# Second block's mixer as one stage: projection in pieces between attention and recurrence, weights through one ring

## Chip, cores and metric

One core of a Trainium2 chip runs the whole program: two transformer blocks of a first model, then one block of a second one, then a norm. The metric is the time of the program on the device in microseconds (us), the median of several executions.

## What is computed

The input is 256 tokens by 1024 features in float32, and all arithmetic is float32. The change touches the mixer of the last block. Cut to what matters:

```python
h = rmsnorm(x, attn_norm)
proj = h @ w_in                               # 1024 x 5400
q, kv, gate, hg_q, hg_f, hg_i, hg_g, merge = split(proj)
# 8 heads of 64, 2 key groups; three branches over all 256 keys or 15 compressed ones
k_cmp, v_cmp = rope(compress(k, w_cmp_k)), compress(v, w_cmp_v)
o_nsa = g0*softmax(q k_cmp)v_cmp + g1*softmax(q k_slc)v_slc + g2*softmax(q k_win)v_win
# gated recurrence, 4 heads, keys and values 128 wide, chunks of 64 tokens
f = lb + (1 - lb) * sigmoid(hg_f);  k = 1 - f;  state = f*state + k v
o_hg = rmsnorm(q . state, hg_norm) * silu(hg_g)
mixed = sigmoid(merge[0]) * (o_nsa @ w_br_nsa) + sigmoid(merge[1]) * (o_hg @ w_br_hg)
x = x + mixed @ w_out
```

A mixture of 32 experts follows, as in the two blocks before it.

## The kernel before

Tokens lie as two tiles of 128 partitions (`TILES`). The program is a row of stages. Each ends in `Stage.close`, which waits for all engines, so nothing of one stage overlaps the next but the loads that a stage issues ahead. A float32 matmul of the program is two matmul instructions in the trace; a transpose is one. PE is TensorE, DVE VectorE, ACT ScalarE, SP the engine that issues the loads.

The mixer is this row of stages in `program`:

- `norm_stage` "s_norm1": `h` and its transpose `hT`. SP loads the first two of twelve 450-column blocks of `w_in` and the two masks `levels` and `causal`, and waits for the masks.
- `project_stage` (matmuls L1115): 12 blocks of columns by 2 tiles by 8 chunks of features, copies out of PSUM by DVE (L1139) and ACT (L1130). Two weight slots.
- `rope_stage` (DVE), `turn_stage` (transposes L1021), `compress_stage` (matmuls L1845) with `Forget` beside it; PE's first transpose there waits for `w_cmp_k` and `w_cmp_v`, loaded in the stage itself.
- `attend_stage`: 12 units (3 branches by 2 tiles by 2 groups of 4 heads). A unit is: scores on PE (L1365), scale and bias on DVE (L1408), row maximum (L1412), exponentials on ACT (L1383), transposes of the probabilities (L1343), their copy by ACT (L1394), the product with v (L1355), then the division and gates on DVE (L1425 to L1434), which sums the branches in SBUF.
- `turn_stage`, then `hgrn_stage`: cumulative sums (L1660, L1663), chunk updates (L1669), seven levels of products within a chunk (L1680) whose factors DVE prepares (L1729, L1730, L1737, L1738) and whose results it masks and adds up (L1747, L1752), then the outputs (L1687, L1692).
- `head_norm_stage`, `turn_stage`, `project_stage` for `w_br_nsa`, again for `w_br_hg`, `turn_stage`, and `project_stage` for `w_out`, which adds to `x` and issues the first loads of the experts.

Of the kernel before, what the change touches and what calls it, by code (L numbers as in the profile page):

```python
# [40 lines left out]
class Stage:  # L41
# [4 lines left out]
    def __init__(self, nc, name):  # L46
        self.nc, self.name, self.sems = nc, name, []
# [677 lines left out]
class NormWeight:  # L725
# [9 lines left out]
    def wait(self, eng):  # L735
        eng.wait_ge(self.landed, 16 * self.n)
# [1142 lines left out]
    arena.at = mark  # L1879


def program(nc, ins, const_dram, out, dump=None):

    psum = nc.alloc_psum_tensor("psum", [P, 4096], F32)
# [14 lines left out]
    def experts_of(tag, names, layer):  # L1899

        stage, mem = Stage(nc, tag), alloc_moe(arena, norm_tile)
        return stage, mem, Experts(stage, mem, extra_slot(arena), *(ins[n][layer] for n in names))
# [6 lines left out]
    def normed(tag, scale=None, shift=None, loads=None, ready_too=None, chunked=False):  # L1909
        norm_stage(nc, tag, x, h, norm_w, scale, shift, hT, ident, banks, loads=loads, ready_too=ready_too, chunked=chunked)  # L1910
# [5 lines left out]
    def ahead_of(plan, w_row):  # L1916
        def loads(sp):
            norm_w.fetch(sp, w_row)
            plan[2].prefetch(sp)
        return loads  # L1920
# [95 lines left out]
        arena.at = 0  # L2016


    mark = arena.at
    arena.take([WEIGHTS])  # L2020
    N = ins["w_in_2"].shape[2]
    in_columns = Columns(nc, "s_in", ins["w_in_2"][0], DC, N // 12, arena, at=mark)
    consts["levels"], consts["causal"] = arena.take([896]), arena.take([TOK])
    later_landed = whole.sem("later_consts")

    def first_loads(sp):
        in_columns.fetch(sp)
        for n in LATER:
            sp.dma_start(consts[n], const_dram[n]).then_inc(later_landed, 16)
        sp.wait_ge(later_landed, 16 * len(LATER))  # L2030

    normed("s_norm1", loads=first_loads)
    out_columns = Columns(nc, "s_out", ins["w_out_2"][0], DC, 512, arena, at=mark)
    nsa_columns = Columns(nc, "s_brn", ins["w_br_nsa_2"][0], DC // 2, 512, arena)
    o = arena.take([TILES, D])
    pr = arena.take([TILES, N])
    project_stage(nc, in_columns, hT, pr, arena, banks)
    kv = pr[:, :, 512:1280].rearrange("p t (s g d) -> p t s g d", s=6, g=2)
    hk, g = arena.take([TILES, 512]), arena.take([TILES, 512])
    mark2 = arena.at  # L2040
    half = ROPE_DIM // 2
    rope = consts["rope"][:, :].rearrange("p (t n) -> p t n", t=TILES)
    heads = lambda ap: ap.rearrange("p (n d) -> p n d", d=64)
    jobs = []
    for t in range(TILES):
        cs = (rope[:, t, 0:half], rope[:, t, half:])
        jobs += [(heads(pr[:, t, 0:512]), *cs), (kv[:, t, 2], *cs), (kv[:, t, 4], *cs)]
    rope_stage(nc, "s_rope", jobs, arena)
    qT, cT = arena.take([HEADS, TOK], parts=64), arena.take([4, TOK], parts=64)
    ksT, kwT = arena.take([2, TOK], parts=64), arena.take([2, TOK], parts=64)  # L2050
    turn_stage(nc, "s_turn", [(pr[:, :, 0:512], 64, 8, qT), (pr[:, :, 512:768], 64, 4, cT), (pr[:, :, 768:896], 64, 2, ksT),
                              (pr[:, :, 1024:1152], 64, 2, kwT)], ident, banks)
    kcT, vc = arena.take([2, N_CMP], parts=64), arena.take([2, 64], parts=N_CMP)
    hq, hf, hi, hg = (pr[:, :, 1304 + i * 512:1304 + (i + 1) * 512] for i in range(4))
    compress_stage(nc, "s_cmp", cT, ins["cmp_pos_2"][0], ins["w_cmp_k_2"][0], ins["w_cmp_v_2"][0], kcT, vc, consts, arena, banks,
                   beside=lambda st: Forget(nc, st, ins["hg_lb_logits_2"], hf, hf, hk, g, (pr[:, :, 1280:1304], pr[:, :, 3352:]),
                                            arena))
    gates = pr[:, :, 1280:1304].rearrange("p t (h i) -> p i t h", i=3)
    cb = consts["cmp_bias"][:, :].rearrange("p (t n) -> p t n", t=TILES)
    cm = consts["cmp_mask"][:, :].rearrange("p (t n) -> p t n", t=TILES)  # L2060
    o_nsa = o[:, :, 0:512]
    nsa = dict(qT=qT, hd=64, kv_of=lambda hh: hh // 4, scale=64 ** -0.5, out=o_nsa)
    some = cm[:, :, 0:1]
    attentions = [dict(nsa, kT=kcT, v=lambda kt, g_: vc[:, g_, :], keys=N_CMP,
                       bias=lambda t, hs, nk: cb[:, t, :].unsqueeze(1).to_broadcast([P, HEADS // 2, N_CMP]),
                       factors=[lambda t, hs: gates[:, 0, t, hs], lambda t, hs: some[:, t, :].to_broadcast([P, HEADS // 2])])]
    for i, (kk, s) in enumerate(((ksT, 3), (kwT, 5))):
        attentions.append(dict(nsa, kT=kk, v=lambda kt, g_, s=s: kv[:, kt, s, g_, :], add=True,
                               bias=lambda t, hs, nk: consts["causal"][:, TOK - nk:].unsqueeze(1).to_broadcast([P, HEADS // 2, nk]),
                               factors=[lambda t, hs, i=i: gates[:, i + 1, t, hs]]))  # L2070
    attend_stage(nc, "s_attn", attentions, ident, arena, psum)
    if dump: dump("s_nsa", o)
    arena.at = mark2
    hqT, hkT = arena.take([HG_HEADS, TOK]), arena.take([HG_HEADS, TOK])
    turn_stage(nc, "s_hturn", [(hq, P, 4, hqT), (hk, P, 4, hkT)], ident, banks)
    o_hg = o[:, :, 512:1024]
    hgrn_stage(nc, "s_hgrn", g, hqT, hkT, hk, hi, o_hg, consts, arena, banks)
    head_norm_stage(nc, "s_hnorm", [(o_hg, 4, 128, ins["hg_norm_2"][0])], arena,
                    loads=lambda sp: (nsa_columns.fetch(sp), out_columns.fetch(sp)), gated=(hg, o_hg))
    arena.at = mark2 - 2 * TILES * 512  # L2080
    turn_stage(nc, "s_oturn", [(o, P, DC, hT)], ident, banks)
    mixed = arena.take([TILES, D])
    hg_columns = Columns(nc, "s_brh", ins["w_br_hg_2"][0], DC // 2, 512, arena)
    tmp = arena.take([TILES, 512])
    project_stage(nc, nsa_columns, hT[:, 0:4, :], mixed, arena, banks, gate=pr[:, :, 3352:3352 + D], ahead=hg_columns.fetch)
    project_stage(nc, hg_columns, hT[:, 4:8, :], mixed, arena, banks, tmp=tmp, gate=pr[:, :, 3352 + D:], add=True)
    turn_stage(nc, "s_mturn", [(mixed, P, DC, hT)], ident, banks)
    arena.at = mark
    plan = experts_of("s_moe", ("w_grp_2", "b_grp_2", "w_rtr_2", "b_rtr_2", "w_gate_2", "w_up_2", "w_down_2"), 0)
    project_stage(nc, out_columns, hT, x, arena, banks, add=True,  # L2090
                  ahead=ahead_of(plan, ins["ffn_norm_2"][0]))
    if dump: dump("s_mix", x)
    arena.at = mark
    normed("s_norm2", loads=extra_of(plan), chunked=True)
    moe(plan, None, ins["final_norm_2"])
    norm_stage(nc, "final", x, h, norm_w, None, None, store=rows(out[0]))
# [55 lines left out]
```

## Time and profile before

| | us |
|---|---|
| median of 3 runs | 2465.34 |
| lowest, highest | 2463.25, 2467.79 |
| the profiled execution's own time | 2461.11 |
| its span | 2459.1 |
| PE busy | 2065.8 |
| DVE busy | 667.0 |
| ACT busy | 358.7 |

The span is counted in the trace from its first to its last record; the execution's own time has 2 us around it. Busy time of PE is summed over the span and does not tell at which of the engine's two clock rates it ran. The three expert stages are the long even stretches of 427 to 430 GB/s in the page; the mixer of the last block lies between the second and third of them, at 1502 to 1946 us.

### The profile page before, as it was taken

To read this page: it belongs to the slowest core of one execution; us is meant where nothing else is said; L and a number is where in the kernel's file an instruction comes from. 1 tells how busy PE (TensorE), PEld (TensorE's weight loads), DVE (VectorE), ACT (ScalarE), POOL (GpSimd) and SP (SyncE) were. 2 spreads that over 40 slices of the span, in tenths; PEclk is the share of its full clock that TensorE was granted. 3 is DMA by queue.
4 is the path that set the end of the run, shared out by engine and by line. 5 is a ranking of instruction groups with operands and counts; after the bars stand their busy time and mean duration, and the time that the engine had idled before them with its cause. 6 is when DMAs were issued, how large, how long until landed. Compare 5 with 4: busy or idle time off the path is not lost. (4 is left out here: it accounts for less than half of the span.)

```text
span 2459.1 us, 29045 instructions
## 1 busy us (share of the span) xinstructions
PE 2065.8 (84%) x11243; PEld 1136.5 (46%) x11243; DVE 667.0 (27%) x1427; ACT 358.7 (15%) x736; POOL 0.3 (0%) x5
## 2 busy tenths in 40 slices
PE   6955689999896967699998886994966789999996
PEld 2634355554443425355554443543853355554442
DVE  2774321111112463411111112004462221111112
ACT  2022121111111012211111101003311121111111
POOL 0000000000000000000000000000000000000000
PEclk9965889999999988699999998996567789999999
DMA  8940949999997953489999993431003749999995
GB/s 290 366 156 11 375 181 422 427 429 427 428 430 291 325 202 146 176 359 428 428 429 428 428 428 142 156 123 27 0 1 138 319 188 423 428 428 428 429 430 243
DMA packets 135016, 732.32 MB, mean 298 GB/s; under 512 B 18736, under 2 KB 44803, under 8 KB 85659
## 3 DMA queue, kind: packets, MB, share of 16 engines
q1 hardware_dynamic: 132860, 728.14, 72.8%
q10 hardware_dynamic: 2080, 3.15, 0.4%
q8 instruction: 50, 0.82, 0.1%
q14 instruction: 26, 0.21, 0.0%
HBM read 727.06 MB, written 4.20 MB: 297 GB/s over the span
## 5 line engine op out<-in xcount | busy, mean ns | idle before, releaser
L261 PE MATMUL psum<-arena,norm_w 128*64 128x256 f32 x6144 | 708.6, 383 | 59.6 <-DMA arena<-in_moe_w_dram 21.1
L261 PEld LDWEIGHTS psum<-arena,norm_w 128*64 128x64 f32 x6144 | 436.1, 137 | 328.1 <-issue 72.1
L292 PE MATMUL psum<-arena,hT 128*64 128x512 f32 x1536 | 349.4, 596 | 22.1 <-DMA arena<-in_moe_w_dram 13.6
L361 DVE COPY hT<-psum 64x512 f32<-64x512 f32 x96 | 66.6, 694 | 780.7 <-PE psum L292 780.7
L1115 PE MATMUL psum<-arena,hT 128*128 128x450 f32 (+1 forms) x640 | 264.3, 575 | 15.9 <-DVEq L1135 15.9
L292 PEld LDWEIGHTS psum<-arena,hT 128*64 128x64 f32 x1536 | 106.1, 136 | 232.8 <-issue 215.8
L1115 PEld LDWEIGHTS psum<-arena,hT 128*128 128x128 f32 x640 | 124.1, 195 | 153.9 <-issue 147.2
L312 PE MATMUL psum<-hT 128*128 128x512 f32 x384 | 177.5, 605 | 2.5 <-ACT hT L361 2.5
L1205 PE MATMUL psum<-arena,hT 128*128 128x290 f32 (+1 forms) x448 | 149.3, 493 | 8.1 <-DMA arena<-in_even_w_in_dram 4.2
L392 ACT ACTIVATE hT<-psum 128x256 f32<-128x256 f32 x96 | 36.8, 383 | 724.6 <-PE psum L261 724.6
L548 DVE COPY hT<-psum 128x256 f32<-128x256 f32 x96 | 40.8, 425 | 322.7 <-PE psum L280 322.7
L1205 PEld LDWEIGHTS psum<-arena,hT 128*128 128x128 f32 x448 | 85.1, 191 | 71.7 <-issue 49.8
L361 ACT COPY hT<-psum 64x512 f32<-64x512 f32 x96 | 55.5, 578 | 413.7 <-PE psum L292 413.7
L312 PEld LDWEIGHTS psum<-hT 128*128 128x128 f32 x384 | 69.0, 189 | 91.3 <-issue 86.2
L691 DVE SCALAR_TENSOR_TENSOR arena<-arena,ccol 128x512 f32<-128x512 f32 x140 | 105.3, 752 | 5.0
L990 PE MATMUL psum<-const_ident,h 128*128 128x128 f32 x80 | 21.7, 433 | 61.3 <-DVEq L977 60.8
L1021 PE MATMUL psum<-const_ident,arena 128*128 128x128 f32 (+1 forms) x174 | 28.2, 335 | 43.5 <-PEq L55 43.5
L384 ACT COPY norm_w<-arena 128x512 f32 x96 | 59.5, 622 | 31.5 <-issue 29.7
L546 DVE TENSOR_TENSOR hT<-hT,psum 128x256 f32<-128x256 f32 x96 | 40.5, 422 | 54.1 <-ACT hT L392 51.2
L1343 PE MATMUL psum<-const_ident,arena 128*128 128x128 f32 (+1 forms) x112 | 25.6, 391 | 30.3 <-ACT arena L1394 24.6
L1365 PE MATMUL psum<-arena 64*128 64x128 f32 (+4 forms) x160 | 46.1, 451 | 4.4 <-PEq L55 4.4
L484 DVE TENSOR_SCALAR arena<-const_iota,arena 128x64 f32<-128x64 f32 x204 | 49.7, 308 | 0.1
(289 smaller groups left out, 1275.0 us busy)
## 6 DMA issues: line engine op xcount, KB each, us to landing
arena<-in_moe_w_dram SPq DMA_DIRECT2D x192, 2048.0 KB, 28.6
arena<-in_w_gate_dram SPq DMA_DIRECT2D x32, 2048.0 KB, 27.8
arena<-in_w_up_dram SPq DMA_DIRECT2D x32, 2048.0 KB
arena<-in_w_down_dram SPq DMA_DIRECT2D x32, 2048.0 KB, 31.7
arena<-in_ada_w_dram SPq DMA_DIRECT2D x24, 2048.0 KB
arena<-in_w_in_dram SPq DMA_DIRECT2D x12, 1800.0 KB, 7.2
arena<-in_odd_w_in_dram SPq DMA_DIRECT2D x6, 2048.0 KB, 13.4
arena<-in_even_w_in_dram SPq DMA_DIRECT2D x8, 1160.0 KB, 14.1
```

The source lines that it names most:

```text
L261: m = nc.tensor.matmul(out[64 * half:64 * half + 64, :], xw[:, u, c, :], w[:, c, half * HALF:(half + 1) * HALF], start=(c == 0), stop=(c = ...
L292: m = nc.tensor.matmul(bank_Y[64 * half:64 * half + 64, :], hTs[:, k % 2, (k // 2) * 64:(k // 2) * 64 + 64], experts.slots[slot][2][:, k, ...
L312: m = nc.tensor.matmul(bank_acc[2 * t + half][:, :], selT[:, t, :], y[:, half, :], start=False, stop=False, skip_group_check=True)
L361: return eng_copy(y[BLOCK * u:BLOCK * (u + 1), half, :], bank_Y[64 * half:64 * half + 64, :])
L384: nc.scalar.copy(xw[:, u], sorted_x[:, :, bass.ds(start, BLOCK)]).then_inc(xw_ready, 1)
L484: m = nc.vector.tensor_scalar(selw[:, t, BLOCK * u:BLOCK * (u + 1)], iota[:, 0:BLOCK], slots[:, t, bass.ds(g, 1)], comb[:, t, bass.ds(g, 1 ...
L546: nc.vector.tensor_tensor(hm, sil, H3[u], ALU.mult).then_inc(hm_ready, 1)
L548: nc.vector.tensor_copy(hTs, HT).then_inc(hT_copied, 1)
L691: m = nc.vector.scalar_tensor_tensor(out, wt[:, k, :], self.ccol[:, k:k + 1], out, ALU.mult, ALU.add)
L1115: m = nc.tensor.matmul(banks[2 * u + t][:, 0:width], inT[:, k, t * P:(t + 1) * P], wt[:, u, k, :], start=(k == 0), stop=(k == kc - 1))
L1205: m = nc.tensor.matmul(banks[2 * u + t][:, 0:width], inT[:, k, t * P:(t + 1) * P], wt[:, b % SLOTS, k, :], start=(k == 0), stop=(k == kc - 1))
L1365: m = nc.tensor.matmul(S(n, nk)[:, i, :], job["qT"][:, h, t * P:(t + 1) * P], job["kT"][:, job["kv_of"](h), 0:nk], start=True, stop=True)
```

## The change

`project_stage`, `rope_stage`, `turn_stage`, `compress_stage`, `attend_stage`, `hgrn_stage`, `head_norm_stage` and their closes are replaced for this mixer by one stage, `second_mixer_stage`. Its weights go through `Ring`: three slots, 11 blocks of `w_in` columns (ten of 512, one of 280), the two branch matrices, two halves of `w_out`. A `project(n, t)` is one block for one tile; in the loops it is cut in two parts of 4 chunks (`QUARTERS`). Queries and keys are transposed two heads at a time (keys are written twice), so that the score matmuls alternate between partitions 0 to 63 and 64 to 127. Gates and division go onto the probabilities before their transpose, the products with v come out transposed, and the three branches add up in one PSUM bank. The two masks and `w_cmp` are loaded in the stage, behind the ring's first three blocks. All copies of projections are ACT's. The diff, cut:

```diff
+IN_2 = ((512, 1024), (0, 512), (1024, 1304), (1816, 2328), (1304, 1816), (2328, 2840), (2840, 3352), (3352, 3864), (3864, 4376),
+        (4376, 4888), (4888, 5400))
+class Ring:
+    SLOTS = 3
...
+    def wait(self, pe, n):
+        pe.wait_ge(self.landed[n % self.SLOTS], 16 * (n // self.SLOTS + 1))
+def second_mixer_stage(nc, ring, x, h, hT, w, consts, arena, psum, banks, ahead):
...
+        def _(sp):
+            sp.dma_start(prow, w["pos"]).then_inc(cw_landed, 16)
+            sp.dma_start(cw[:, 0], w["cmp_k"].rearrange("(l d) o -> d l o", d=64)).then_inc(cw_landed, 16)
+            sp.dma_start(cw[:, 1], w["cmp_v"].rearrange("(l d) o -> d l o", d=64)).then_inc(cw_landed, 16)
...
+            for n in range(ring.SLOTS, OUT + 1):
+                sp.wait_ge(made[1], n - ring.SLOTS + 1)
+                ring.load(sp, n)
+            sp.wait_ge(brn_made, 4)
+            ring.load(sp, OUT + 1)
+            sp.wait_ge(mix_ready, 4)
+            ahead(sp)
...
+            pe.wait_ge(cw_landed, 48)
+            nc.tensor.transpose(banks[2][0:64, 0:CMP_LEN], prow, ident[0:CMP_LEN, 0:CMP_LEN]).then_inc(pos_turned, 1)
+            project(0, 0)
+            project(0, 1)
+            project(1, 0)
...
+            def score(u):
...
+                for j in range(4):
+                    rows = slice(64 * (j % 2), 64 * (j % 2) + 64)
+                    m = nc.tensor.matmul(S[:, (j % 2) * 2 + j // 2, 0:nk], qT[rows, 2 * s + j // 2, t * P:(t + 1) * P],
+                                         kT[rows, s, 0:nk], start=True, stop=True)
...
+            def turn_unit(u):
...
+                pe.wait_ge(normed, u + 1)
...
+            pe.wait_ge(exped, 1)
+            for n in range(len(UNITS) + 3):
+                if n >= 3:
+                    output_unit(n - 3)
+                if 2 <= n < len(UNITS) + 2:
+                    turn_unit(n - 2)
+                if n < len(UNITS):
+                    score(n)
+                project(*QUARTERS[n])
+            project(*QUARTERS[len(UNITS) + 3])
+            pe.wait_ge(decayed, 1)
+            pe.wait_ge(o_kept, 4)
...
+            for n in range(len(LEVELS) + 1):
+                compare(n)
+                project(*QUARTERS[16 + n])
+            project(*QUARTERS[23])
+            pe.wait_ge(ready, 1)
...
+        def _(act):
...
+            for n in range(len(UNITS) + 2):
+                if n >= 2:
...
+                    act.wait_ge(turned, n - 1)
...
+                    nc.scalar.copy(PT[0:wd, n % 2, 0:k, :], T[0:wd, 0:k, :]).then_inc(pt_copied, 1)
+                if n < len(UNITS):
...
+                    act.wait_ge(maxed, n + 1)
...
+                if n >= 2 and n % 2 == 0:
+                    keep(*QUARTERS[n - 1][0:2])
+            keep(*QUARTERS[13][0:2])
+            keep(*QUARTERS[15][0:2])
+            for n in range(len(LEVELS)):
+                act.wait_ge(asked, n + 1)
...
+        def _(dve):
...
+            for n in range(len(UNITS) + 3):
+                if n < len(UNITS):
+                    scale(n)
+                if 1 <= n < len(UNITS) + 1:
+                    normalise(n - 1)
+                if n >= 3 and (n - 3) % 3 == 2:
+                    keep_output((n - 3) // 3)
...
+            for n in range(last + 2):
+                if n + 1 < last:
+                    exponents(n + 1)
+                if n < last:
+                    factors(n)
+                if n == 0:
+                    carry()
+                if n:
+                    collect(n - 1)
...
-    project_stage(nc, in_columns, hT, pr, arena, banks)
...
-    attend_stage(nc, "s_attn", attentions, ident, arena, psum)
...
-    hgrn_stage(nc, "s_hgrn", g, hqT, hkT, hk, hi, o_hg, consts, arena, banks)
...
+    ring = Ring(nc, "s_mix", loads, arena, 0)
+    normed("s_norm1", loads=ring.fetch)
...
+    second_mixer_stage(nc, ring, x, h, hT, dict(
...
+        hg_norm=ins["hg_norm_2"][0], levels=const_dram["levels"], causal=const_dram["causal"]), consts, arena, psum, banks, ahead)
```

How PE's instructions stand around two attention units of 256 keys. In the kernel before, L1365 are scores, L1343 transposes, L1355 products with v:

```order
L1365 MATMUL psum<-arena 128x256 x4
L1355 MATMUL psum<-arena 128x64 x4
L1343 MATMUL psum<-const_ident,arena 128x128 x4
L1365 MATMUL psum<-arena 128x256 x4
L1355 MATMUL psum<-arena 128x64 x4
L1343 MATMUL psum<-const_ident,arena 128x128 x8
```

In the changed kernel, L2101 are scores, L2114 transposes, L2130 products with v and L2025 the projection:

```order
L2025 MATMUL psum<-arena,hT 128x512 x4
L2130 MATMUL psum<-arena 64x128 x8
L2114 MATMUL psum<-const_ident,h 15x128 x4
L2101 MATMUL psum<-arena 128x256 x4
L2025 MATMUL psum<-arena,hT 128x512 x4
L2130 MATMUL psum<-arena 64x128 x4
L2114 MATMUL psum<-const_ident,h 128x128 x8
```

Every round now holds four matmuls of 128x512, and the transposes come one round later behind the scores.

On PE in the recurrence, before: sums' updates (L1669), all levels in a row (L1680), first output:

```order
L1669 MATMUL psum<-arena 128x128 x12
L1680 MATMUL psum<-arena 128x128 x56
L1687 MATMUL psum<-arena 128x128
L1692 MATMUL psum<-arena 64x128
```

Now, with L2151 the updates and L2164 the levels:

```order
L2151 MATMUL psum<-arena 128x128 x12
L2164 MATMUL psum<-arena 128x128 x8
L2025 MATMUL psum<-arena,hT 128x512 x4
L2164 MATMUL psum<-arena 128x128 x8
L2025 MATMUL psum<-arena,hT 128x512 x4
L2164 MATMUL psum<-arena 128x128 x8
```

Between two levels there are again four matmuls of the projection.

On SP at the start of the mixer, now: three blocks in the norm stage, then what the stage itself loads before its first block is released:

```order
L1903 DMA arena<-in_w_in_dram 128x8x512 x2
L1903 DMA arena<-in_w_in_dram 128x8x280
L943 UNCONDITIONAL_BRANCH
L1996 UNCONDITIONAL_BRANCH
L1998 DMA arena<-in_cmp_pos_dram 32x64
L1999 DMA arena<-in_w_cmp_k_dram 64x32x64
L2000 DMA arena<-in_w_cmp_v_dram 64x32x64
```

The compression weights stood in a stage of their own after the whole projection; they now stand behind three blocks of the projection in the queue.

## Rows read from the trace of the kernel before

**Rows 1.** The page: busy tenths of PE and its clock in 40 slices.

```profile
PE   6955689999896967699998886994966789999996
PEclk9965889999999988699999998996567789999999
```

**Rows 2.** Stretches: us, busy of PE, PEld, DVE, ACT, POOL, clock, DMA share, GB/s.

```profile
1516.80:1665.00 148.20, 148.12 (x384) 73.77 (x384) 6.90 (x11) 5.87 (x11) 0.00 (x0) 0.98 0.36 125
1665.00:1690.00 25.00, 5.29 (x33) 4.45 (x33) 8.10 (x41) 10.11 (x10) 0.00 (x0) 0.72 0.45 61
1690.00:1710.00 20.00, 7.40 (x259) 6.93 (x258) 16.26 (x25) 3.40 (x3) 0.00 (x0) 0.50 0.01 5
1710.00:1788.00 78.00, 74.20 (x288) 62.65 (x288) 28.80 (x69) 29.14 (x109) 0.00 (x0) 0.50 0.00 1
...
1795.00:1868.00 73.00, 40.58 (x196) 33.17 (x196) 48.81 (x66) 14.37 (x18) 0.00 (x0) 0.66 0.09 32
...
1874.00:1910.00 36.00, 29.36 (x64) 12.59 (x64) 7.93 (x12) 0.00 (x0) 0.00 (x0) 0.95 0.27 104
...
1914.00:1945.40 31.40, 29.59 (x64) 12.85 (x64) 2.58 (x4) 0.00 (x0) 0.00 (x0) 0.93 0.92 356
sum 428.60, PE 344.33 PEld 215.09 DVE 124.66 ACT 66.39 POOL 0.00; mean PE 34.43 PEld 21.51 DVE 12.47 ACT 6.64 POOL 0.00
```

**Rows 3.** The same view at two loads: first blocks with masks, then w_cmp.

```profile
1503.00:1515.00 12.00, 3.81 (x16) 2.85 (x16) 4.04 (x7) 4.57 (x9) 0.00 (x0) 0.50 0.98 356
1681.00:1690.00 9.00, 0.16 (x1) 0.12 (x1) 0.00 (x0) 5.74 (x4) 0.00 (x0) 0.60 1.26 168
```

**Rows 4.** Timeline of PE, the compression: start, us, group, idle before.

```profile
1689.84 0.26 PE L1840 MATMUL psum<-const_ident,arena 32*64 32x32 f32 x1 [11.81 <-DMA arena<-in_w_cmp_v_dram]
1694.37 7.02 PE L1845 MATMUL psum<-arena 64*15 64x64 f32 x256 [4.28 <-DVEq L1862]
```

**Rows 5.** Groups by shape, attention of the last block: busy us, mean ns, idle before.

```profile
L1383 ACT ACTIVATE arena<-arena 128x256 f32<-128x256 f32 x16 | 7.9, 497 | 19.1 <-DVE arena L1412 19.1
L1408 DVE SCALAR_TENSOR_TENSOR arena<-psum,arena 128x1024 f32<-128x1024 f32 x4 | 4.9, 1225 | 12.5 <-PE psum L1365 12.5
L1394 ACT COPY arena<-psum 128x1024 f32<-128x1024 f32 x4 | 4.0, 1000 | 7.7 <-PE psum L1343 7.7
```

**Rows 6.** Attention of the second block (heads of 128): its clock, then PE's timeline.

```profile
936.00:954.00 18.00, 12.04 (x88) 10.90 (x88) 8.27 (x12) 8.69 (x30) 0.00 (x0) 1.00 0.00 1
...
936.71 1.89 PE L1365 MATMUL psum<-arena 128*128 128x256 f32 x8
...
943.84 1.06 PE L1343 MATMUL psum<-const_ident,arena 128*128 128x128 f32 x8 [2.18 <-ACT arena L1394]
...
948.49 3.74 PE L1355 MATMUL psum<-arena 128*128 128x128 f32 x32
```

**Rows 7.** Timeline of PE: one row half at a time, row halves in turn, column halves in turn.

```profile
1747.90 2.07 PE L1365 MATMUL psum<-arena 64*128 64x128 f32 x8
...
221.03 2.24 PE L1528 MATMUL psum<-arena 64*128 64x128 f32 x16 [4.11 <-DVEq L1570]
...
1439.47 3.67 PE L261 MATMUL psum<-arena,norm_w 128*64 128x256 f32 x32 [1.08 <-DMA arena<-in_moe_w_dram]
```

**Rows 8.** The recurrence: DVE's first and last of the levels, PE's last two levels.

```profile
1806.93 0.69 DVE L1729 TENSOR_TENSOR arena<-arena 128x512 f32<-128x512 f32 x1
...
1837.72 3.84 PE L1680 MATMUL psum<-arena 128*128 128x128 f32 x32 [0.98 <-DVEq L1739]
...
1844.58 1.23 DVE L1752 TENSOR_TENSOR arena<-arena 128x1024 f32<-128x1024 f32 x1
```

**Rows 9.** Timeline of PE: the turn after the head norm, the second branch.

```profile
1868.62 3.65 PE L1021 MATMUL psum<-const_ident,arena 128*128 128x128 f32 x16 [12.16 <-PEq L55]
...
1892.43 13.97 PE L1115 MATMUL psum<-arena,hT 128*128 128x512 f32 x32 [2.60 <-DVEq L1135]
```

More of the change, by code:

```diff
@@ L1879, in compress_stage, with __init__, tile, load @@
     arena.at = mark
+IN_2 = ((512, 1024), (0, 512), (1024, 1304), (1816, 2328), (1304, 1816), (2328, 2840), (2840, 3352), (3352, 3864), (3864, 4376),
+        (4376, 4888), (4888, 5400))
+class Ring:
+    SLOTS = 3
+    def __init__(self, nc, tag, loads, arena, at):
+        self.stage, self.loads = Stage(nc, tag), loads
+        self.wt = arena.view([self.SLOTS, DC * 512], at, P)
+        self.landed = [self.stage.sem(f"w{u}") for u in range(self.SLOTS)]
+    def tile(self, n, kc, width):
+        return self.wt[:, n % self.SLOTS, 0:kc * width].rearrange("p (c n) -> p c n", c=kc)
+    def load(self, sp, n):
+        src = self.loads[n]
+        kc, width = src.shape[0] // P, src.shape[1]
+        sp.dma_start(self.tile(n, kc, width), src.rearrange("(c p) n -> p c n", p=P)).then_inc(self.landed[n % self.SLOTS], 16)
+    def fetch(self, sp):
+        for n in range(self.SLOTS):
+            self.load(sp, n)
+    def wait(self, pe, n):
+        pe.wait_ge(self.landed[n % self.SLOTS], 16 * (n // self.SLOTS + 1))
@@ L2016, in program @@
         arena.at = 0
[L2019 to L2036, printed above, removed]
-    project_stage(nc, in_columns, hT, pr, arena, banks)
[L2038 to L2070, printed above, removed]
-    attend_stage(nc, "s_attn", attentions, ident, arena, psum)
-    if dump: dump("s_nsa", o)
-    arena.at = mark2
-    hqT, hkT = arena.take([HG_HEADS, TOK]), arena.take([HG_HEADS, TOK])
@@ L2075, in program @@
-    turn_stage(nc, "s_hturn", [(hq, P, 4, hqT), (hk, P, 4, hkT)], ident, banks)
-    o_hg = o[:, :, 512:1024]
-    hgrn_stage(nc, "s_hgrn", g, hqT, hkT, hk, hi, o_hg, consts, arena, banks)
[L2078 to L2089, printed above, removed]
@@ L2090, in program, with ahead @@
-    project_stage(nc, out_columns, hT, x, arena, banks, add=True,
-                  ahead=ahead_of(plan, ins["ffn_norm_2"][0]))
+    w_in = ins["w_in_2"][0]
+    loads = [w_in[:, a:z] for a, z in IN_2] + [ins["w_br_nsa_2"][0], ins["w_br_hg_2"][0]]
+    loads += [ins["w_out_2"][0][:, i * 512:(i + 1) * 512] for i in range(2)]
+    ring = Ring(nc, "s_mix", loads, arena, 0)
+    normed("s_norm1", loads=ring.fetch)
+    arena.at = ring.SLOTS * DC * 512
+    plans = []
+    def ahead(sp):
+        at, arena.at = arena.at, 0
+        plans.append(experts_of("s_moe", ("w_grp_2", "b_grp_2", "w_rtr_2", "b_rtr_2", "w_gate_2", "w_up_2", "w_down_2"), 0))
+        arena.at = at
+        ahead_of(plans[0], ins["ffn_norm_2"][0])(sp)
```

506 lines of the change are left out of this document (505 added, 1 removed).

## The prediction

> **What bounds the kernel now.** I read the page's slices first [rows 1]: each is 61.5 us, and while experts run PE has 8 or 9 tenths and nearly full clock. In the 28th to 32nd slice, 1660 to 1967 us, it has 4, 9, 6, 6 and 7 tenths, and the clock 6, 5, 6, 7 and 7. Next the stretches of that mixer [rows 2]. From its first projection matmul at 1516.8 us to DVE's last add at 1945.4 it takes 428.6 us; PE is busy in 344.3 of them, DVE in 124.7, ACT in 66.4. No other engine is near PE, so two things can be won: the 84.3 us in which PE idles, and the part of its busy time that only a low clock makes. The clock column shows where that is. The projection has 0.98 (1.2 and 2.4 GHz are the two levels, 0.5 and 1.0): 148.12 us for 2 tiles of 5400 columns. Compression and attention stand at 0.50, where PE is "busy" 74.2 of 78 us; the recurrence has 0.66, with PE busy 40.6 of 73 and DVE 48.8. Branches and output again have 0.93 to 0.95. DMA has a share of 0.36 in the projection's stretch, so weights do not bound it.
>
> That attention's busy time is clock and not work is seen in the second block, where the granted clock was 1.00 although PE was busy only 12.0 of 18 us [rows 6]: there eight score matmuls of 128x256 take 1.89 us, eight transposes 1.06, 32 products of 128x128 3.74. Those are my prices at full clock: 0.24, 0.13 and 0.12 us an instruction.
>
> **The change, part by part.** I cost it as PE's list in order of time, at full clock, with the waits that stay; DVE and ACT are the cover to be tested.
>
> *Start.* Before, the norm stage waits for two blocks and the masks: 356 GB/s over 12 us, 4.27 MB [rows 3]. Now it fetches three blocks, 5.3 MB, and waits for none. But PE's first instruction waits for `w_cmp` behind them. In the kernel before, those loads held PE 11.8 us [rows 4], most of it in a stretch where 168 GB/s were moved for 9 us [rows 3]. At that pace I put about 8.5 us behind the ring's blocks, which themselves take some 15 us from 1502.5: PE begins at 1526 instead of 1516.8. Bounds: 1521 if the two kinds of load share the queues' time, 1530 if they run one after the other at the old wait's 11.8. The cost is 9 us, open from 4 to 13.
>
> *Phase 1, blocks 0 to 4.* Their projection is 2328 of the 5400 columns: 2328/5400 x 148.1 = 63.9 us [rows 2]. Moved between them: 42 transposes at 0.13 = 5.5; compression, 256 instructions in 7.0 as before [rows 4]; the cumulative sums 3.7 (16 instructions of 128 columns at 0.12, four of 512 at the 0.437 of 13.97/32 [rows 9]); 2.3 waiting for their exponentials on ACT (one pass of 1024 columns takes 1.0, as the copy L1394 does [rows 5]); 1.5 for a dip of the clock at the small compression matmuls. Sum 84. The rope, the forget gate and the copies hide under 8-matmul groups of 7 us; the separate stages from 1665 to 1710, 45 us of which PE used 12.7, and their closes disappear.
>
> *Phase 2, attention.* 14 rounds up to the last output, each with a quarter of four 128x512 matmuls, hence two instructions each: 8 x 0.437 = 3.5 [rows 9], 14 x 3.5 = 49.1. Work of attention: 64 transposes x 0.13 = 8.3; outputs, 128 instructions of 128 columns, 11.5; scores 12. The last two have bounds. Scores in one row half at a time took 2.07 us for 8 instructions of 128 columns at half clock, so 0.13 at full, and 256 columns twice that; with row halves in turn 16 took 2.24, 0.14 each at half clock [rows 7]: alternation nearly halves it. All pairs overlapping gives 7.7, none 15.4; I take the middle, as only one layout of two is alike. Outputs alternate column halves; the nearest row, 32 of 256 columns in 3.67, is 0.115 each [rows 7], which says overlap; 0.06 for 128 columns gives 8, no overlap 15.4, and I take 11.5. Sum 81, bounds 75 to 88.
> Beside it the Trainium skill, page "TensorE: Matmul & The Clock Gate", section "Part 3: Packing small matmuls — row/col tiling", says that matmuls in different row groups run at the same time, their weight loads overlapping. By that rule scores would be 7.7 and this phase 4 us shorter; the trace agrees for row halves with 0.14 against 0.26.
>
> What covers it: at 256 keys DVE needs scale 1.22, maximum 1.22, normalisation (a pass of 1024 like them) 1.23 and three small ones of some 0.2, together 4.3; ACT four exponentials of 0.50 and a copy of 1.0, and half a copy of a projection [rows 5]. The score of unit n is followed by a quarter and an output before the transposes that wait for the normalisation of unit n-1: 3.5 + 1.4 = 4.9 us of PE. So DVE is hidden by about 0.6 us, in the four units of 256 keys only; the eight smaller units have over 1.5. The fetch of a 2.1 MB block, 5.9 us at the 356 GB/s of [rows 3], hides under the 14 us that a block's matmuls last.
>
> *Phase 3, recurrence.* Two quarters 7.0, updates 24 at 0.12 = 2.8; seven levels and the diagonal. In each, 16 instructions; 32 of them took 3.84 at the better clock [rows 8], so 1.92 a level, 13.4 for seven; eight quarters 28.1; 2 waiting for DVE. Sum 53. DVE's levels from first to last took 38.9 [rows 8], partly waiting for ACT and PE; per level DVE has four passes of 0.69 and two masks and an add, about 5.4, as much as PE's 1.92 + 3.5. This cover is thin as well, hence the 2.
>
> *Phase 4.* Last products of the recurrence, 40 at 0.12 = 4.8; first branch 14.0; 4 transposes and a copy 1.4; second branch 14.0 [rows 9]; turn and copies 2.3; output 28.0; second turn 1.0; add 0.8. Sum 66.3. The head norm, where PE idled 12.2 us before L1021 [rows 9], now runs on ACT and DVE under the first branch, about 14 us against 14: the cover just reaches. The experts' first loads still start some 31 us ahead of the end, as before at 1914, so the next stage keeps its start.
>
> Sum 84 + 81 + 53 + 66.3 = 284.3, and 3 us for some thirty hand-overs among engines that I did not price singly. 1526 + 287.3 = 1813.3, against 1945.4: 132.1 us less. Of these about 84 are idle time, less the 9 of the start and 7 of waits that stay, and the other 60-odd are PE's work at full instead of half clock. The profiled execution's own time was 2461.1 and becomes 2329.0; the median of the runs is 4.2 above it, so the forecast is **2333**.
>
> **Rivals.**
> *B, the hand-overs bind.* PE waits in each round for DVE's normalisation or ACT's copy, as it waited 2.18 us for L1394 even at full clock [rows 6]. For it: covers of 0.6 us, and `link` waits between DVE's small operations. Against: only four units are of 256 keys. Price 2.18 x 12 = 26: 2359.
> *C, the clock stays at 1.2 GHz in part of the rounds.* For it: all attention of this mixer ran at 0.50 although PE was busy 95% of the time [rows 2], and rounds of this kind alternate banks and wait. Against: the second block's attention had 1.00 with gaps [rows 6], and half of each round is the projection that had 0.98. If half of phase 2 is at half clock, 40 us: 2373. The Trainium skill, same page, section "A second HAM failure mode: psum-queue depth-cycling", describes a clock that falls again and again in a kernel that cycles PSUM banks; by it the time would be this one.
> *D, the other side.* Interleaving pulls the projection down with attention instead of the reverse: phases 2 and 3 wholly at half clock. Their 134 us double; the gain of 132 is gone and the kernel takes 2467 or a little more. It decides from 132 us of PE's work at half rate. Against it speaks the same row of the projection, and that PE has fewer gaps than before.
> *E, it doesn't do what it says.* Blocks arrive late from a ring of three and PE stands at every block, so that the work is still serial: about 2465. It takes 12 us lateness per block; the fetch rate of [rows 3] says 5.9 us for each.
>
> **Chances.** Forecast 0.62, own range 2318 to 2350 (start 4 to 13, phase 2 75 to 88, some 8 us either way on thin covers). B 0.20, C 0.13, D 0.03, E 0.02. The range reaches down to 2313, as all terms at their low ends give, and up through B and C to 2385; about 0.1 lies outside, D and E among it. A measurement of this kernel can tell about 0.2%, 5 us, from no change: A, B and C are all faster, 0.95; E is the same, 0.02; D slower, 0.03.
>
> **What would show it.** PE's first instruction of the stage at 1526 right after a wait for `w_cmp`. A clock of 1.0 from the first block to some 1810, with at most a dip at compression. Rounds of 7 to 8 us around units of 256 keys, and of 5 to 6 around others, with idle PE below 0.3 us in each; B would show as idle before the transposes with DVE's normalisation as what ended it, C as quarters of 7 us and not 3.5. Levels of 5.4 to 5.8 us. The first branch without a gap behind it, and the stage's last add at about 1813. The forecast is wrong if this add comes after 1830 or the clock in the rounds lies under 0.8.

## The result and the profile after

The changed kernel takes 2325.5 us, the median of four executions, against 2464.9: the ratio is 0.943, interval 0.941 to 0.945. One of the four took 6232 us; nothing in the later runs is like it, its cause is not known, and it is left out of the ratio, though not out of the median (the other three have 2321.7). Timed once more beside another kernel it took 2317.4 (0.941, 0.939 to 0.942), so 139 to 145 us are saved, where 132 had been forecast. The profiled execution took 2329.4.

The page of the changed kernel, busy tenths of PE and its clock in 40 slices (now 58.2 us each), answers to [rows 1]:

```profile
PE   7955769999988696768999988869999799999886
PEclk9975769999999898869999999979999799999999
```

The mixer lies in the 27th to 32nd slice (from 1513 us). The clock has 7 tenths in the first of them, with the wait at the start, 9 in the four after it, and 7 in the last, most of which lies behind the mixer. The stretches by the four phases of the prediction answer to [rows 2] (same columns):

```profile
1537.42:1620.70 83.28, 78.82 (x480) 42.18 (x480) 23.55 (x52) 16.83 (x27) 0.00 (x0) 0.96 0.38 136
1620.70:1697.45 76.75, 76.75 (x400) 40.11 (x401) 32.96 (x70) 32.99 (x117) 0.00 (x0) 1.00 0.24 84
1697.45:1748.97 51.52, 49.67 (x218) 29.72 (x217) 35.70 (x50) 8.27 (x10) 0.00 (x0) 1.00 0.23 82
1748.97:1815.75 66.78, 64.47 (x193) 30.61 (x191) 16.70 (x25) 13.60 (x16) 0.00 (x0) 1.00 0.59 226
sum 278.33, PE 269.71 PEld 142.62 DVE 108.91 ACT 71.69 POOL 0.00; mean PE 67.43 PEld 35.65 DVE 27.23 ACT 17.92 POOL 0.00
```

From PE's first instruction to DVE's last add the mixer lasts 278.3 us where it had lasted 428.6. PE idles 8.6 of them and not 84.3, and is busy 269.7 and not 344.3, half the gain each way: 75.7 us of idle time and 74.6 of busy time. The clock is 1.00 through attention and recurrence, where it had been 0.50 and 0.66. DVE is busy 15.8 us less than before (108.9 us) and ACT 5.3 more (71.7); their work now lies beside PE's.

The timeline of PE in the changed kernel (start, us, group, idle before) at the stage's start, in the rounds around units of 256 keys, and in the levels:

```profile
1519.35 3.81 PE L990 MATMUL psum<-const_ident,h 128*128 128x128 f32 x16 [11.89 <-DVEq L977]
1537.42 0.25 PE L2039 MATMUL psum<-const_ident,arena 32*64 32x32 f32 x1 [14.26 <-DMA arena<-in_w_cmp_v_dram]
...
1580.67 1.41 PE L2058 MATMUL psum<-arena 64*15 64x64 f32 x87 [2.20 <-issue]
...
1620.70 0.62 PE L2101 MATMUL psum<-arena 64*128 64x15 f32 x8 [2.26 <-ACT arena L2269]
...
1661.29 0.66 PE L2130 MATMUL psum<-arena 128*64 128x128 f32 x8
1661.88 0.61 PE L2114 MATMUL psum<-const_ident,h 128*15 128x128 f32 x4
1662.42 1.13 PE L2101 MATMUL psum<-arena 64*128 64x256 f32 x8
1663.48 3.70 PE L2025 MATMUL psum<-arena,hT 128*128 128x512 f32 x8
1667.11 0.65 PE L2130 MATMUL psum<-arena 15*64 15x128 f32 x8
1667.70 1.09 PE L2114 MATMUL psum<-const_ident,h 128*128 128x128 f32 x8
...
1714.11 2.05 PE L2164 MATMUL psum<-arena 128*128 128x128 f32 x16 [1.03 <-DVEq L2468]
1716.00 3.60 PE L2025 MATMUL psum<-arena,hT 128*128 128x512 f32 x8
1719.44 1.95 PE L2164 MATMUL psum<-arena 128*128 128x128 f32 x16
...
1821.31 4.89 PE L990 MATMUL psum<-const_ident,h 128*128 128x128 f32 x16 [6.28 <-DVEq L977]
```

Read it so: after the norm's transposes PE waits 14.3 us for the load of `w_cmp`, then runs without a gap but for 2.2 us in the middle of the compression matmuls, for which the profile shows no cause, 2.3 at the first scores, 0.8 and 1.0 in the levels, and 0.3 and 1.3 behind the branches. From one round's products to the next it is 5.8 us in the rows shown, and 5.8 to 6.7 in the four rounds with scores of 256 keys, with no idle time shown. The distance from the norm's first transpose (L990) to that of the next norm is the measure used below: it holds the mixer with both its ends, 302.0 us here, 302.3 in the second profile of the same kernel, and 444.5 in the kernel before (1506.94 to 1951.41). So the stage gives 142.5 us. In the first profile it merely began 12.4 us later than before; in the second, 2.2 us later (1509.10). Those 10 us are the difference between the two executions (2329.4 and 2319.6). They arise in the earlier stages, which are the same in all kernels here, and in whose profiles the norm begins anywhere from 1502.6 to 1519.4 us; what causes that is not known.

### The profile page after: what moved, and what is told of

Read it like the earlier page. It is cut to its first block and busy times, and to the rows that moved or that the text cites. A ratio compares the mean times of both kernels' runs of the same rounds, so it can differ in the third digit from the quotient of the medians.

```text
span 2327.6 us, 28443 instructions
## 1 busy us (share of the span) xinstructions
PE 2002.0 (86%) x11195; PEld 1070.3 (46%) x11195; DVE 651.3 (28%) x1387; ACT 364.0 (16%) x748; POOL 0.3 (0%) x5
## 5 line engine op out<-in xcount | busy, mean ns | idle before, releaser
L2025 PE MATMUL psum<-arena,hT 128*128 128x512 f32 (+1 forms) x352 | 154.8, 590 | 0.0
L1205 PEld LDWEIGHTS psum<-arena,hT 128*128 128x128 f32 x448 | 86.0, 193 | 72.5 <-issue 51.3
L2025 PEld LDWEIGHTS psum<-arena,hT 128*128 128x128 f32 x352 | 65.8, 194 | 69.0 <-issue 66.8
L990 PE MATMUL psum<-const_ident,h 128*128 128x128 f32 x80 | 21.7, 434 | 60.2 <-DVEq L977 59.8
L1115 PE MATMUL psum<-arena,hT 128*128 128x512 f32 x128 | 57.3, 609 | 3.5 <-DVEq L1135 3.5
L716 PE MATMUL psum<-arena,const_ones 128*128 128x512 f32 x40 | 24.3, 773 | 26.1 <-PEq L55 26.1
L990 PEld LDWEIGHTS psum<-const_ident,h 128*128 128x128 f32 x80 | 14.3, 217 | 69.7 <-DVEq L977 69.7
## 6 DMA issues: line engine op xcount, KB each, us to landing
arena<-in_odd_w_in_dram SPq DMA_DIRECT2D x6, 2048.0 KB, 13.1
```

What stands on the lines that cost most here:

```text
L1115: m = nc.tensor.matmul(banks[2 * u + t][:, 0:width], inT[:, k, t * P:(t + 1) * P], wt[:, u, k, :], start=(k == 0), stop=(k == kc - 1))
L1205: m = nc.tensor.matmul(banks[2 * u + t][:, 0:width], inT[:, k, t * P:(t + 1) * P], wt[:, b % SLOTS, k, :], start=(k == 0), stop=(k == kc - 1))
L2025: m = nc.tensor.matmul(banks[t][:, 0:width], hT[:, k, t * P:(t + 1) * P], ring.tile(n, DC, width)[:, k, :], start=(k == 0), stop=(k == DC ...
```

## Experiments

All are edits of the changed kernel. "Stage" is the distance between the two norms' first transposes, 302 us in the changed kernel.

**The projection taken out of the rounds.** Three kernels: everything ahead of the attention; only the levels alone; only the attention alone.

```diff
+            for q in range(0, 24):
+                project(*QUARTERS[q])
             pe.wait_ge(exped, 1)
             for n in range(len(UNITS) + 3):
...
-                project(*QUARTERS[n])
-            project(*QUARTERS[len(UNITS) + 3])
...
-                project(*QUARTERS[16 + n])
-            project(*QUARTERS[23])
```

(ACT's copies moved in the same way; in the second kernel quarters 16 to 23 stand ahead of the updates, in the third quarters 0 to 15 ahead of the attention.)

> All of the projection stands before the attention, nothing of it between rounds or levels. Theory 1 (the gain is that the chains of DVE and ACT run beside the projection, and the clock stays up because PE is never idle): attention alone takes some 55 us with PE idle for a third or more of it, the recurrence some 40, so the stage grows by 55 - 28 + 40 - 16 = about 50 us, 2375. Theory 2 (the clock alone: attention by itself keeps PE busy, only at 1.2 GHz): attention stands at clock 0.5 with PE busy over 90%, about 56 us, and the recurrence loses little: 2355. Theory 3 (the merged stage and the new layout make the gain, interleaving little): within 10 us of the changed kernel, 2335 or less.

> Projection between the attention rounds as in the change, but the last eight quarters ahead of the levels. Theory 1: levels are bound by DVE's 5.4 us a level, 40 us for seven with PE idle 3 of each 5, against 16 beside the projection: the stage from its first matmul to DVE's last add grows from 278 to about 300 us. Theory 3: by under 5 us.

> Sixteen quarters ahead of the attention, the last eight between the levels. Theory 1: the stage grows from 278 to about 305 us, attention takes about 55 us, and the two losses (this one and that of the levels alone) add up to that of the kernel with everything first. Theory 2: attention at clock 0.5 and PE busy over 90%. In both the clock recovers in the levels.

Everything first: 2383.0 us, ratio 0.967 (0.966 to 0.969), stage 363.6, 61.6 more. Levels alone: 2344.3, stage 329.4, 27.4 more. Attention alone: 2360.7, stage 337.7, 35.7 more; the two add up to 63 (these two, and all kernels below but those of the start, were executed once, so I compare them by their stage). Stretches of the kernel with everything first, attention and then the levels, columns as above:

```profile
1692.44:1757.41 64.97, 42.81 (x289) 31.03 (x289) 30.89 (x69) 28.91 (x109) 0.00 (x0) 0.66 0.09 33
...
1757.41:1792.19 34.78, 23.53 (x136) 21.77 (x136) 31.62 (x46) 13.68 (x11) 0.00 (x0) 0.71 0.00 0
```

And PE's timeline there, at the end of the projection and the first rounds, then around units of 256 keys:

```profile
1609.94 82.56 PE L2025 MATMUL psum<-arena,hT 128*128 128x512 f32 x192
...
1696.45 0.61 PE L2114 MATMUL psum<-const_ident,h 128*15 128x128 f32 x4 [2.25 <-DVE h L2424]
1696.99 1.21 PE L2101 MATMUL psum<-arena 64*128 64x128 f32 x8
...
1718.34 2.08 PE L2101 MATMUL psum<-arena 64*128 64x256 f32 x8
...
1730.43 1.97 PE L2114 MATMUL psum<-const_ident,h 128*128 128x128 f32 x8 [3.07 <-DVE h L2424]
```

From its first scores to the updates the attention takes 65.0 us by itself. In the change the same stretch is 83.8 us with 16 quarters in it. A quarter takes 3.44 us when they stand in a row (82.56 for 24), which leaves 28.8: 36.2 are lost. PE idles 22.2 of them, 18.6 before transposes, for DVE's normalisation, and 2.4 for ACT's copies; the other 14 are its own instructions at a low clock (scores of 256 keys 2.08 us for 1.13, transposes 1.97 for 1.09). So neither theory holds alone. Idle time comes first and the clock follows: the first scores of 128 keys still take 0.71 us, and those behind the first wait of 2.25 us take 1.21. The mean is 0.66, between the two levels, not the 0.50 with PE over 90% busy that theory 2 wanted. Theory 1 had the right places, and the two parts add up nearly as it said, but it was 12 us short because it counted the clock at nothing. In the kernel with the levels alone it is the same: PE waits 0.5 to 4.5 us before each level, and the first branch behind them takes 16.1 us for 14.0. Theory 3, taken alone, is out: interleaving gives 61.6 of the stage's 142.5 us. But the larger part, 81 us, stays with everything first, and belongs to the merged stage and the new layout. Held point by point against the kernel before,

```profile
1710.30 3.56 PE L1365 MATMUL psum<-arena 64*128 64x15 f32 x16 [1.53 <-PEq L55]
...
1806.90 4.11 PE L1669 MATMUL psum<-arena 64*128 64x128 f32 x24 [6.00 <-DVEq L1719]
...
1846.02 0.49 PE L1687 MATMUL psum<-arena 128*128 128x128 f32 x2 [4.45 <-DVEq L1777]
```

22 of the 81 lie ahead of the first scores, 32 from there to the updates, under 1 in the levels, and 27 from the recurrence's outputs to the next norm. Apart from the row halves below, no run takes these 81 us apart into closes, moved work and layout.

**Half as much per round, and the same in lumps.** In one kernel each round has two chunks of a projection (blocks 5 and 6 ahead of the attention), in the other two quarters in every second round.

```diff
-                project(*QUARTERS[n])
-            project(*QUARTERS[len(UNITS) + 3])
+                project(*EIGHTHS[n], 2)
+            project(*EIGHTHS[len(UNITS) + 3], 2)
```

```diff
-                project(*QUARTERS[n])
-            project(*QUARTERS[len(UNITS) + 3])
+                if n % 2 == 0:
+                    project(*QUARTERS[n])
+                    project(*QUARTERS[n + 1])
```

> Each round of attention has half as much projection (1.75 us for 3.5), the rest stands ahead of the attention. If idle time alone counts, small units stay hidden (cover 1.75 + 1.3 against DVE's 2.3), units of 256 keys expose 1 to 2 us each, the stage grows by 4 to 8 us at clock 1.0. If the clock needs the dense rounds, attention falls to a clock under 0.8 and the stage grows by 15 or more.

> Two quarters of projection in every second round of attention and none in the others, the same work in all. Rounds without projection have only scores, transposes and products to cover DVE's 2.3 to 4.3 us: if it is the even spreading that hides the chain, PE waits 1 to 3 us in six of the rounds, the stage grows by 6 to 12 us. If the queues even this out over two rounds, by under 2. The clock stays at 1.0 in either case.

Half as much: 2326.2, stage 305.6, 3.6 more, with 4.8 us of PE waiting in five rounds and a clock of 0.95 over the attention: near the first of my two cases, though I had put the clock at 1.0 there. In lumps: 2340.6, stage 323.6, 21.6 more. The attention of the lumps, from the first scores to the updates, and two places behind a round without projection:

```profile
1608.35:1716.36 108.01, 94.57 (x416) 49.31 (x416) 35.88 (x75) 32.78 (x117) 0.00 (x0) 0.89 0.17 60
```

```profile
1664.97 1.03 PE L2114 MATMUL psum<-const_ident,h 128*15 128x128 f32 x4 [2.73 <-DVE h L2433]
1665.94 2.08 PE L2101 MATMUL psum<-arena 64*128 64x256 f32 x8
1667.94 7.28 PE L2025 MATMUL psum<-arena,hT 128*128 128x512 f32 x16
...
1695.48 1.91 PE L2114 MATMUL psum<-const_ident,h 128*128 128x128 f32 x8 [3.54 <-DVE h L2433]
```

Of the 24.2 us by which 108.0 exceeds the changed kernel's 83.8 for the same work, 13.4 are idle and 10.8 slower instructions: even with as much projection in all, PE waits up to 3.5 us in the rounds without projection, and what comes behind the waits of 2.7 and 3.5 us shown runs at the low clock. (These rounds also hold small matmuls only. This pair of kernels does not part the wait from that mix; the doubled maximum below shows a slower quarter behind a wait in rounds that kept their projection, at one place.) My expectation that the clock stays at 1.0 was wrong, and it is why over 20 us were lost and not at most 12. (The stage grows by 21.6 and not 24.2 because a dip of the clock at the compression, told of below, is missing in this profile and PE's stop there is shorter. The same holds for the kernels with half as much and with the attention alone, so that all three lose 2.6 to 2.9 us more than their stages say.) Even spreading is worth more than the amount: half the work in every round costs 3.6 us, all of it in every second round 21.6.

**How thin DVE's cover is.**

```diff
+                if nk == 2 * P:
+                    nc.vector.tensor_reduce(rtmp[:, 0, 4 * u:4 * u + 4], L[:, u % 2, :, 0:nk], AX.X, ALU.max, negate=True)
                 nc.vector.tensor_reduce(mx[:, u % 3], L[:, u % 2, :, 0:nk], AX.X, ALU.max, negate=True).then_inc(maxed, 1)
```

> DVE takes the row maximum of the four units of 256 keys twice (the second result is not used), 1.2 us more each. In the changed kernel the transposes of two units start 0.07 us after their normalisation ends, one 0.9 us after it, one over 1. If the cover is as thin as that, PE waits in total 2 to 3 us before transposes and the stage grows by as much, from 302 to 304.5. If the cover is the 0.6 us that the prediction gave each round, 2.4 us spread over four. If PE's queue hides more, nothing.

2324.4 us; the stage 303.6. DVE's timeline in the changed kernel first, the unit of 256 keys whose transposes (L2114) PE begins at 1667.70; then PE's in this one:

```profile
1663.60 1.23 DVE L2418 SCALAR_TENSOR_TENSOR h<-psum,arena 128x1024 f32<-128x1024 f32 x1 [2.60 <-PE psum L2101]
1664.86 1.22 DVE L2420 TENSOR_REDUCE arena<-h 128x4 f32<-128x1024 f32 x1
1666.00 0.17 DVE L2428 RECIPROCAL arena<-arena 128x4 f32<-128x4 f32 x1
1666.20 0.17 DVE L2429 TENSOR_TENSOR arena<-arena 128x4 f32<-128x4 f32 x1
1666.40 1.23 DVE L2432 TENSOR_TENSOR h<-h,arena 128x1024 f32<-128x1024 f32 x1
```

```profile
1650.44 0.61 PE L2114 MATMUL psum<-const_ident,h 128*15 128x128 f32 x4 [0.22 <-DVE h L2434]
...
1657.36 1.09 PE L2114 MATMUL psum<-const_ident,h 128*128 128x128 f32 x8 [1.03 <-DVE h L2434]
1658.38 0.62 PE L2101 MATMUL psum<-arena 64*128 64x15 f32 x8
1658.93 5.36 PE L2025 MATMUL psum<-arena,hT 128*128 128x512 f32 x8
...
1678.92 1.09 PE L2114 MATMUL psum<-const_ident,h 128*128 128x128 f32 x8 [1.04 <-DVE h L2434]
```

1666.40 + 1.23 is 1667.63, and PE's transposes begin 0.07 us later: the cover is just used up in two rounds of fifteen. In the other two units of 256 keys 2.5 and 3.3 us lie between them, more than I wrote ahead of the run. With 1.2 us more on DVE PE waits 2.29 us in three places, 1.03 and 1.04 of them in those two. Behind the first of these the quarter takes 5.36 us for 3.70. From first score to updates that gives 88.0 us for 83.8, of which 2.3 is waiting and 1.7 the clock. The stage grows by 1.6 only, for the dip at the compression is missing here too, and PE's stop there is 1.3 us shorter.

**The row halves of the scores.** First only the order, then all in one half.

```diff
-                for j in range(4):
+                for j in (0, 2, 1, 3):
```

```diff
-                    rows = slice(64 * (j % 2), 64 * (j % 2) + 64)
+                    rows = slice(0, 64)
```

> Score matmuls in the order of heads 0, 2, 1, 3, so that two with the same row half stand together, where the change has the halves in turn. If two matmuls in different row halves run at the same time, the eight instructions of a unit of 256 keys go from 1.14 us to 1.5 to 1.9 and all scores from 9.9 us to 12 to 14; the stage grows by 3. If the order doesn't matter: 1.14 us, no difference.

> All score matmuls read partitions 0 to 63, so that heads 1 and 3 of each group get the queries of heads 0 and 2: this leaves out half of the scores' own data, and the number and shape of the matmuls stay. If matmuls in different row halves run at the same time (and the order 0, 2, 1, 3 merely kept enough of that), the eight instructions of 256 keys go from 1.14 to about 1.9 us, those of 128 from 0.72 to 1.05, and the stage grows by 4. If the price follows from the shape alone: no difference.

The order changes nothing in the scores: 2322.5, stage 301.2, scores of 256 keys still 1.14 us. (The stretch from first scores to updates is 1.8 us longer by a slower first quarter, and the dip at the compression is missing.) One half alone: 2332.7, stage 310.9, 9.0 more. PE's scores there, of 15, 128 and 256 keys, to be held against 0.62, 0.71 and 1.13:

```profile
1648.61 1.06 PE L2101 MATMUL psum<-arena 64*128 64x15 f32 x8
...
1642.73 1.16 PE L2101 MATMUL psum<-arena 64*128 64x128 f32 x8
...
1654.41 1.99 PE L2101 MATMUL psum<-arena 64*128 64x256 f32 x8
```

Four units of each: 4 x (1.06 + 1.16 + 1.99) = 16.8 us for 9.9. The second row half is worth 7 us at full clock. Most of the other 2 us is a quarter at 5.40 us for 3.70, behind the 2.3 us wait before the first scores. The Trainium skill, "TensorE: Matmul & The Clock Gate", "Part 3: Packing small matmuls — row/col tiling", has matmuls in different row groups run concurrently; by that rule these scores were to halve, and the trace comes near it with 0.57 to 0.62 of the time.

**The head norm laid bare.**

```diff
+            for t in range(TILES):
+                pe.wait_ge(hg_normed, t + 1)
...
             ring.wait(pe, BRN)
...
-            for t in range(TILES):
-                pe.wait_ge(hg_normed, t + 1)
```

> PE turns the head norm's result before the first branch and not behind it. In the changed kernel DVE delivers the two halves 7.1 and 8.6 us after PE's last product of the recurrence. Shown bare, this costs 8 to 9 us between those products and the first branch, and the clock may dip; the stage grows by 8 to 10. If the head norm were no limit, under 2.

2332.7, stage 311.1, 9.2 more, nearly all of it behind the recurrence's last product: PE waits 7.08 and 0.45 us before the transposes, and the branch begins at a low clock.

```profile
1756.09 1.11 PE L2187 MATMUL psum<-const_ident,arena 128*128 128x128 f32 x4 [7.08 <-DVEq L2524]
1757.65 1.12 PE L2187 MATMUL psum<-const_ident,arena 128*128 128x128 f32 x4 [0.45 <-DVEq L2524]
1758.56 14.70 PE L2195 MATMUL psum<-arena 128*128 128x512 f32 x32
```

The branch that covers it in the changed kernel lasts 14.0 us and needs to last 8.6: the prediction's "about 14 us against 14: the cover just reaches" saw too little cover.

**The start.** The wait for `w_cmp` behind three half blocks of projection; then also ACT's copy of block 0 ahead of its wait for the forget gate's logits.

```diff
-            pe.wait_ge(cw_landed, 48)
-            nc.tensor.transpose(banks[2][0:64, 0:CMP_LEN], prow, ident[0:CMP_LEN, 0:CMP_LEN]).then_inc(pos_turned, 1)
             project(0, 0)
             project(0, 1)
             project(1, 0)
+            pe.wait_ge(cw_landed, 48)
+            nc.tensor.transpose(banks[2][0:64, 0:CMP_LEN], prow, ident[0:CMP_LEN, 0:CMP_LEN]).then_inc(pos_turned, 1)
```

```diff
+            for t in range(TILES):
+                keep(0, t)
             act.wait_ge(lb_asked, 1)
             nc.scalar.activation(lb, lb, ACT.Exp).then_inc(lb_exped, 1)
-            for n in range(3):
+            for n in range(1, 3):
                 for t in range(TILES):
                     keep(n, t)
```

> PE's wait for w_cmp and the little transpose behind it stand after three half blocks of projection. The changed kernel idles 14.3 us before that transpose. If only this wait held PE, it starts on block 0 as soon as the block has landed, 8 to 12 us earlier, and the time falls to about 2315. Rival: the three blocks of the ring share the queues and land together some 15 us after the start of the fetch, near 1529 in the changed kernel's count: then 8 us are gained at most and PE waits for the ring.

> As the kernel with the w_cmp wait moved behind three half blocks, and ACT keeps block 0 before it waits for the forget gate's logits. In the kernel e4 PE idled 6.3 us before its third half block, waiting for ACT's copy, and ACT stood in its wait for the logits (17.4 us). If that wait is the cause, the 6.3 us go and the time falls 5 to 8 us below e4's 2311, to 2305. Rival: the copy was late for the w_cmp transfer's sake, and PE now idles as long at the transpose for w_cmp: 2311.

> The changed kernel unchanged, timed beside the next one. Its first executions spread from 2318 to 2329; the norm before the stage began 12 us later in the profiled one than in the kernel before. If that is chance and not the change, the stage alone accounts for 142 us and the median falls between 2318 and 2325, a ratio of 0.941 to 0.943; if something makes the part before the mixer slower, every profile shows the 12 us.

The change timed again gave 2317.4 and 0.941; its profile has the part before the mixer 10.3 us shorter than the first one, so the change does not cause the 12 us. The median lies just below the 2318 to 2325 expected.

With the first edit 2311.2 us, 0.938 (0.937 to 0.940), stage 296.7. PE starts 1.5 us after the norm's transposes, 9.8 us after SP issues the first block, so block 0 has landed by then and the rival, which had all three land some 15 us after the start, falls. But the two projections of block 0 fill both banks, and a new wait appears; PE's rows, then DVE's and ACT's that explain it:

```profile
1507.53 13.97 PE L2025 MATMUL psum<-arena,hT 128*128 128x512 f32 x32 [1.50 <-PEq L55]
1527.82 9.58 PE L2025 MATMUL psum<-arena,hT 128*128 128x512 f32 x16 [6.32 <-ACT arena L2239]
```

```profile
1524.10 0.69 DVE L2352 TENSOR_TENSOR arena<-arena 128x512 f32<-128x512 f32 x1 [17.86 <-DMA arena<-in_hg_lb_logits_dram]
...
1526.14 1.06 ACT L2242 ACTIVATE arena<-arena 128x1024 f32<-128x1024 f32 x1 [17.37 <-DVEq L2354]
```

ACT's first instruction is the exponential of the logits, and their load stands behind `w_cmp` in SP's queue. So PE starts 13.1 us earlier, but the stage gains 5.3 and not the 8 to 12 expected: 6.3 go into the new wait, and the half block behind it takes 9.58 us for 7.03. With the second edit both waits are gone and the stage is 288.3, 13.7 less than the change: 2305.0 us, 0.937 (0.936 to 0.938), against 2317.4 for the change timed beside it. PE's start in this kernel:

```profile
1507.57 3.81 PE L990 MATMUL psum<-const_ident,h 128*128 128x128 f32 x16 [11.90 <-DVEq L977]
1512.89 22.45 PE L2025 MATMUL psum<-arena,hT 128*128 128x512 f32 x48 [1.50 <-PEq L55]
1535.27 0.22 PE L2042 MATMUL psum<-const_ident,arena 32*64 32x32 f32 x1
```

This version beats both kernels. It needs no faster load, only that nobody waits for a late one before there is need.

## Why the prediction came out as it did

It was right in mechanism, and 10 us too cautious. Against the stage's own 142.5 us it had 132.1. The first median, 2325.5, lies within its 2318 to 2350, and the later one, 2317.4, just below. By its terms:

| term | forecast | measured |
|---|---|---|
| later first instruction | +9 | +8.2 (18.07 after the norm's first transpose, 9.87 before) |
| phase 1 | 84 | 83.3 |
| phase 2 | 81 | 76.8 |
| phase 3 | 53 | 51.5 |
| phase 4 | 66.3 | 66.8 |
| hand-overs not priced singly | 3 | within the phases |

- *Start.* The sum of two transfers one behind the other was right. That it was the largest avoidable wait I did not say; the last experiment got back 13.7 us.
- *Phase 1* met its sum, with one wait that I had not priced: the 2.2 us in the middle of the compression matmuls.
- *Phase 2* was the mis-sized term, and within its bounds of 75 to 88 (its own low ends, 49.1 + 8.3 + 7.7 + 8, add up to 73 and not 75). Rounds with scores of 256 keys took 5.8 to 6.7 us where I had named 7 to 8. Scores took 9.9 us for 12 and outputs 9.6 for 11.5: for both I had taken the middle between all pairs overlapping and none, though [rows 7] showed overlap in both forms. The rule cited there would have put the scores at 7.7 and the phase at 77; the phase took that, but with the outputs' help, since the scores came to 9.9. The rounds hand over within the overlap of PE's own instructions, so no 3 us for hand-overs show there.
- *Cover by DVE* in units of 256 keys: forecast 0.6 us in four, measured 0.07 in two, and 2.5 and 3.3 in the others. It held, barely. I had set the same PE time against every round; in fact a round that has the 15-key outputs ahead of 256-key transposes has the least cover.
- *Rival B* (hand-overs bind) was less than 1.2 us of DVE away in two units: the doubled maximum shows it. *Rival C* (a low clock in half of the rounds) did not happen in this order of work, and happened at once in the lumps, 0.89 with 10.8 us of slower instructions. What B and C took from the kernel before is not fully answered: its attention stood at 0.50 with PE busy 74.2 of 78 us [rows 2], so it stayed low there with hardly any waits, and no run shows why. *Rival D* would have needed the projection pulled down to the lower level throughout; in the rounds its quarters took 3.6 to 3.7 us. *E*: no wait for a block of the ring shows in the profile.
- The split of the gain was said as about 68 us of idle time and 60-odd of low clock; measured are 67.5, with the 8.2 of the start taken off, and 74.6. What the prediction did not part is the gain of merging and layout, 81 us, from that of interleaving, 61.6. "PE's work at full instead of half clock" is not all of the second: some 7 us of it are the row halves.
- The forecast for the profiled execution, 2329.0, met 2329.4 by two errors that cancel: the stage was 10 us shorter, and that execution reached it 12 us later than the kernel before did, by chance. So the near match is luck.

## What to carry to other kernels

Where an engine idles in short waits and its clock is low, look for independent work of its own to lay between the waits, in pieces as long as the other engines' chain for one round, and in every round: with none in the attention the stage lost 35.7 us, with the same work in every second round still 21.6, and with half of it in every round 3.6. Then look at what stands first in each engine's list of such a merged stage. Here PE and ACT each began with a wait for a load late in the queue, which cost 14 us; work whose data had already landed was standing behind them.

## What the runs showed of the chip that was not expected

- A wait of 1.0 to 2.3 us can cost another 1.7 us: the quarter behind it takes 5.36 to 5.40 us for 3.70. It does not always happen. Behind the 2.26 us wait at the first scores the changed kernel showed none in two profiles, while the kernels with the other score order, with one row half and with the lumps did.
- In the middle of the 256 compression matmuls PE stops for 0.9 to 2.5 us in all thirteen profiles of the changed kernel and its edits, with nothing named as the cause; the kernel before has no such row (7.02 us for all 256 [rows 4]). Behind the stop the next group takes 8.8 to 9.2 us for 7.1 in eight profiles, with stops of 1.0 and 1.4 to 2.5 us, and 7.13 in five, with stops of 0.9 to 1.3. Stop and dip together move the first phase between 80.4 and 84.0 us. The rest repeats closely: first scores to updates is 83.81 or 83.82 us in five profiles of kernels in which it is the same. What sets off stop and dip was not settled.
- Score matmuls in two row halves take 1.13 us whether the halves alternate at each head or only once in four; I had expected the order to matter.
- Scores of 15 keys are as dear as those of 128 (1.06 and 1.16 us for eight in one row half), and both gain from a second half.
